# Modulation columns and first norm moved ahead of table work, and four short convolutions moved from TensorE to VectorE

## Chip, cores and metric

The kernel runs on one core of a Trainium2 chip. The metric is the device time of one execution in microseconds. TensorE (PE in the profile) does matrix products, VectorE (DVE) and ScalarE (ACT) elementwise work, GpSimd (POOL) elementwise work in SBUF, and SyncE (SP) issues most DMAs. Each runs its own queue of instructions in order and meets the others at semaphores.

## The reference

A 512-token sequence of width 1024 passes through three layers: a first block whose mixer is half S5 state space and half gated delta rule, followed by a routed mixture of experts; then a recurrent and windowed-attention layer and a Mamba-2 layer, each with a convolutional feed-forward part. The change lies at the start of the first block:

```python
mod = silu(c) @ w_ada + b_ada
sh1, sc1, gt1, sh2, sc2, gt2 = split(mod, 6)
a_in = rmsnorm(h, norm1_g) * (1 + sc1) + sh1
proj = a_in @ w_in
u_s5, qkv, z, a_gate, b_gate = split(proj, ...)

# S5, for each of its 2048 states
lam_bar = exp(lam * exp(log_step))
b_bar = (lam_bar - 1) / lam * b
states = scan(x -> lam_bar * x + b_bar u)
y = real(c states) + d_skip * u

# gated delta rule
qkv = silu(causal_depthwise_conv(qkv, conv_w))   # width 4, 1536 channels
q, k = l2norm(q) * 128 ** -0.5, l2norm(k)
```

## The kernel before

Activations lie with features on the partitions: h and u are 8 tiles (k = 0 to 7) of 128 features by the tokens. All weights of dense products come as units of 1 MB (16 blocks of 128x128) through a ring of four slots; SP loads a unit when the one that had its slot is used up (`load_unit`, L363). The order of work is written out by hand, one program per engine, and semaphores tie them together.

**The head, up to the first projection.** TensorE sums the squares of h for the norm (L497), then makes the first third of the modulation vector from eight units (`mod_unit`, L517) as rows; ScalarE copies them out (L1238) and TensorE transposes them (`mod_turned`, L524). VectorE meanwhile computes the S5 constants, a tile [128, 16] for each, then tables of the powers of the rotation, `fine` (16 entries, four doublings) and `coarse` (8 entries, three doublings), L1792 to L1813. After them it raises `s5_angle` to 2, which releases GpSimd (L2443). It then scales C into `cl5` (L1817 to L1828) and raises `s5_angle` to 3. Only then does it wait for `mod_turned` (L1831), add the bias (`mod_columns`), form the gain `modg`, and run `norm_apply(0, ...)`: for each k one scalar_tensor_tensor (L1681) and one tensor_scalar (L1675), with a drain between, one k overlapped with the next. Each k raises `normed`, and TensorE's first projection tile waits for each k (`out_tile`, L489). Last comes `bl_build(0)`, which makes four shifted versions of B for the first four S5 tiles.

GpSimd, from `s5_angle` 2 on, makes the sine and cosine tables of steps 0 and 1 (L2467 to L2475), then `cl_build` (the next four powers on C, L2450 to L2453), then the table of step j when VectorE has finished step j - 2.

**The projections.** TensorE does the four tiles of u_s5 with their reorder (`u4_turn`, L547), the gate columns (L562), and then 16 steps j. Step j: projection tile NS5 + j (12 tiles of q, k, v, then 4 of z), a convolution for 1 <= j <= PE_CONV, the S5 input product `s5_in` (L583), the turn of B for the next step `b4_turn` (L574), one unit of the rest of the modulation vector (L517), and in some steps an l2 sum (L623), `d4_in` (L594, in steps 2, 6, 10, 14) and `s5_out` (L610, in steps 4, 8, 12). VectorE's step j: a convolution for PE_CONV <= j < 12, the S5 scan of tile j (two TENSOR_TENSOR_SCAN at L1901 and ten products and sums around them), `bl_build` of the next four tiles in steps 1, 5 and 9, and `s5_result` in steps 5, 9, 13.

**The two ways of the convolution.** With i below PE_CONV (4) ScalarE first builds four diagonal 128x128 matrices of the taps (`conv_taps`, L1243) and copies the projection tile into the padded buffer `cbuf`; TensorE convolves by four matmuls with the shifted buffer (`conv_out`, L617) back into the tile's PSUM bank, and ScalarE takes the silu from there (L1248). With i from 4 on VectorE convolves, one tensor_scalar and three scalar_tensor_tensor (`conv`), and ScalarE takes the silu in place in SBUF (L1252). In both a square for the l2 norm follows when i < 8 (L1258). The lines that choose:

```python
if 1 <= j <= PE_CONV:                   # TensorE
    conv_out(j - 1)
...
if PE_CONV <= j < 12:                   # VectorE
    dve.wait_ge(sem("tile_read"), q0 + NS5 + j + 3)
    conv(qkv[:, j, :], cbuf[j % 2], CONV_C, ...)
```

A projection tile has one of two pairs of PSUM banks, and the tile after next needs its bank read (`tile_read`): by the silu for a tile that TensorE convolves, by the copy into `cbuf` for the others.

Of the kernel before, what the change touches and what calls it, by code (L numbers as in the profile page):

```python
# [26 lines left out]
ACT = mybir.ActivationFunctionType  # L27
AX = mybir.AxisListType.X

P = 128  # L30
# [34 lines left out]


CONV_C = 4
PE_CONV = 4
CONV_F = 3
LRU = 8  # L70
Q_HEADS = 16
# [105 lines left out]
def program(nc, a):  # L177
    with ExitStack() as ctx:
# [1024 lines left out]
        def _(act):  # L1203
# [90 lines left out]
            act.wait_ge(sem("pads_ready"), 1)  # L1294
            for j in range(16):
                q = q0 + NS5 + j
                if j == PE_CONV:
                    conv_silu(j - 1)
                act.wait_ge(sem("tile_done"), q + 1)
                if j < 12:  # L1300
                    if 2 <= j < PE_CONV + 2:
                        act.wait_ge(sem("conv_done"), j - 1)
                    if j >= PE_CONV + 2:
                        act.wait_ge(sem("conv_v"), j - PE_CONV - 1)
                    act.activation(cbuf[j % 2][:, 3:], pair(q), ACT.Copy
                                   ).then_inc(sem("conv_in" if j < PE_CONV else "tile_read"), 1)
                else:
                    act.activation(z1[:, j - 12, :], pair(q), ACT.Silu).then_inc(sem("tile_read"), 1)
                if j == 0:
                    b4_read(0)  # L1310
                if j + 1 < S5_TILES:
                    b4_read(j + 1)
                if 1 <= j < 13 and j != PE_CONV:
                    conv_silu(j - 1)
                if j + 1 >= 2 and j + 1 < PE_CONV:
                    conv_taps(j + 1)
                if j % 4 == 3:
                    d4_read(j // 4)
                if j == 11:
                    act.wait_ge(sem("squares_used"), DT + 8)  # L1320
                    act.wait_ge(sem("norm_applied"), 1)
                    act.activation(l2r, ps[0:8, 1, 0:SEQ], ACT.Sqrt, bias=eps[0:8, :]).then_inc(sem("l2_read"), 1)
# [315 lines left out]
            for n in range(len(SSD) + 3):  # L1638
                if n < len(SSD):
                    c, g = SSD[n]  # L1640
                    cnt, b = CH2[c][1], n % 2
                    act.wait_ge(sem("scan_in_done"), 16 + n + 1)
                    if n >= 2:
                        act.wait_ge(sem("scan_out_done"), 4 + n - 1)
                    bank = ps[:, 2 * b, :].rearrange("p (h n) -> p h n", h=4)
                    d = decay2[b][0:cnt, :, 0:cnt]
                    for e in range(4):
                        act.activation(d[:, e, :], bank[0:cnt, e, 0:cnt], ACT.Relu, scale=-1.0,
                                       bias=cs2[0:cnt, c, 4 * g + e:4 * g + e + 1])
                    if c:  # L1650
                        act.activation(eg2[b][:, :, 0:cnt], bank[:, :, 0:cnt], ACT.Exp).then_inc(sem("conv_in"), 1)
                    act.drain()
                    act.activation(d, d, ACT.Exp, scale=-1.0).then_inc(sem("scan_decay"), 1)
                if n >= 3:
                    group_square(n - 3)
# [17 lines left out]
        def _(dve):  # L1673
# [115 lines left out]
            for _ in range(2):  # L1789
                dve.drain()  # L1790
                doubled()
            for tab, size in ((fine, 16), (coarse, 8)):  # L1792
                dve.memset(tab[0][:, :, 0:1], 1.0)
                dve.memset(tab[1][:, :, 0:1], 0.0)
                n = 1
                while n < size:
                    dve.drain()
                    wc, ws = (S(x).unsqueeze(2).broadcast_to([P, S5_TILES, n]) for x in (15, 16))
                    t = [at(2048 + 256 * x, S5_TILES * n).rearrange("p (j n) -> p j n", n=n) for x in range(4)]
                    tt(t[0], tab[0][:, :, 0:n], wc, mul)  # L1800
                    tt(t[1], tab[1][:, :, 0:n], ws, mul)
                    tt(t[2], tab[0][:, :, 0:n], ws, mul)
                    tt(t[3], tab[1][:, :, 0:n], wc, mul)
                    tt(S(17), S(15), S(15), mul)
                    tt(S(18), S(16), S(16), mul)
                    tt(S(19), S(15), S(16), mul)
                    dve.drain()
                    tt(tab[0][:, :, n:2 * n], t[0], t[1], sub)
                    tt(tab[1][:, :, n:2 * n], t[2], t[3], add)
                    tt(S(15), S(17), S(18), sub)  # L1810
                    ts(S(16), S(19), 2.0, None, mul)
                    n *= 2
                dve.drain()  # L1813
            dve.drain().then_inc(sem("s5_angle"), 1)
            dve.wait_ge(sem("weights_loaded"), WEIGHTS)
            wide = lambda x: x.unsqueeze(2).broadcast_to([P, S5_TILES, 32])
# [10 lines left out]
                    ts(cl5[1][:, :, 0, :], t1, -1.0, None, mul)  # L1827
                dve.drain()  # L1828
            dve.drain().then_inc(sem("s5_angle"), 1)

            dve.wait_ge(sem("mod_turned"), 1)  # L1831
            def mod_columns(t0, tiles):

                turned = ps[:, 3, 256:256 + P].rearrange("p (o h r) -> p h r o", o=2, h=2)[:, :, 0:tiles // 2, :]
                out = mod[:, t0:t0 + tiles].rearrange("p (r o) -> p r o", o=2)
                tt(out, turned[:, 0], pcol("b_ada", t0, tiles).rearrange("p (r o) -> p r o", o=2), add)
                dve.drain()
                tt(out, turned[:, 1], out, add).then_inc(sem("mod_read"), 1)

            mod_columns(0, 16)  # L1840
            dve.drain()
            stt(modg[:, 0:DT], mod[:, DT:2 * DT], 1.0, pcol("norm1_g", 0, DT), add, mul)
            dve.drain()
            norm_apply(0, lambda k: modg[:, k:k + 1], lambda k: h[:, k, META:T2], lambda k: u[:, k, 0:SEQ], SEQ,
                       lambda k: mod[:, k:k + 1])

            def bl_build(t):

# [592 lines left out]
        def _(pool):  # L2441
# [98 lines left out]
            for n in range(len(CH2) * SSD_G + 2):  # L2540
                if n < len(CH2) * SSD_G:
                    c, g = n // SSD_G, n % SSD_G
                    (lo, cnt), b = CH2[c], n % 2
                    if n >= 2:
                        pool.wait_ge(sem("scan_out_done"), 4 + n - 1)
                    pool.wait_ge(sem("scan_scaled"), 16 + n + 1)
                    m = pool.tensor_tensor(xdd[0:cnt, b], xdt[n % 3][0:cnt], tail2[0:cnt, c, 4 * g:4 * g + 4].unsqueeze(2).broadcast_to(  # L2547
                        [cnt, 4, HEAD]), ALU.mult)
                    if c:
                        pool.wait_ge(sem("conv_in"), PE_CONV + n - SSD_G + 1)  # L2550
                        C = xbc[:, SSD_X + SSD_G + g, lo:lo + cnt]
                        m = pool.tensor_tensor(cdec[b][:, :, 0:cnt], eg2[b][:, :, 0:cnt], C.unsqueeze(1).broadcast_to([P, 4, cnt]),
                                               ALU.mult)
                    m.then_inc(sem("scan_pool"), 1)
# [145 lines left out]
```

## Time and profile before

| | |
|---|---|
| three runs | 3108.88, 3109.65, 3119.19 us |
| median | 3109.65 us |
| profiled execution | 3110.36 us |
| its span | 3108.5 us |
| TensorE busy | 2854.5 us, 92% |
| VectorE busy | 1035.6 us, 33% |
| ScalarE busy | 620.8 us, 20% |
| GpSimd busy | 268.8 us, 9% |

The span runs from the first to the last instruction of the profiled execution; 1.9 us of its time lie around it. Starts in rows are us from the span's beginning. A line in a row can be that of a helper: L1678 is VectorE's tensor_tensor, L1675 its tensor_scalar, L1681 its scalar_tensor_tensor, L489 every dense product of TensorE. The granted clock of TensorE is given as a share of full speed; 1.00 is 2.4 GHz and 0.50 is 1.2 GHz. The name `work` stands for the large buffer in which most tiles lie, `tmp` holds the padded buffers `cbuf`. A row of the order in time merges instructions of one form; its us run from the first one's start to the last one's end, and [16.50 <-DVE u L1675] says how long the engine was idle before it and who released it.

### The profile page before, as it was taken

To read this page: it belongs to the slowest core of one execution; us is meant where nothing else is said; L and a number is where in the kernel's file an instruction comes from. 1 tells how busy PE (TensorE), PEld (TensorE's weight loads), DVE (VectorE), ACT (ScalarE), POOL (GpSimd) and SP (SyncE) were. 2 spreads that over 40 slices of the span, in tenths; PEclk is the share of its full clock that TensorE was granted. 3 is DMA by queue.
4 is the path that set the end of the run, shared out by engine and by line. 5 is a ranking of instruction groups with operands and counts; after the bars stand their busy time and mean duration, and the time that the engine had idled before them with its cause. 6 is when DMAs were issued, how large, how long until landed. Compare 5 with 4: busy or idle time off the path is not lost.

```text
span 3108.5 us, 37906 instructions
## 1 busy us (share of the span) xinstructions
PE 2854.5 (92%) x14859; PEld 2136.6 (69%) x14859; DVE 1035.6 (33%) x2148; ACT 620.8 (20%) x1304; POOL 268.8 (9%) x368
## 2 busy tenths in 40 slices
PE   4999887678994999999999999999989899999998
PEld 2554683423332886687888788888877687888787
DVE  6355642311114342604333201113437604333202
ACT  1121220101112453602111001111127402111000
POOL 3121220011220000000000000000006400000000
PEclk7999998689997998999999999999978899999999
DMA  5133102478963111011212122122210011212122
GB/s 226 69 123 122 55 1 122 160 293 356 377 246 126 68 67 56 2 68 55 79 70 73 62 108 108 60 76 68 81 41 2 1 68 58 78 67 81 54 109 81
DMA packets 49449, 312.15 MB, mean 100 GB/s; under 512 B 12192, under 2 KB 14496, under 8 KB 18336
## 3 DMA queue, kind: packets, MB, share of 16 engines
q1 hardware_dynamic: 39520, 290.28, 24.5%
q0 software_dynamic: 9216, 17.85, 1.5%
q8 instruction: 98, 1.61, 0.2%
q10 hardware_dynamic: 576, 2.10, 0.2%
q14 instruction: 39, 0.32, 0.0%
HBM read 351.08 MB, written 16.78 MB: 118 GB/s over the span
## 4 chain that ended last, share of the span: by engine, by line
PE 65%; DVE 2%; ACT 1%; issue 0%; DVEq 0%; POOL 0%; POOLq 0%; ACTq 0%
PE ps L489 35%; PE ps L1001 18%; PE ps L1044 2%; PE ps L966 1%; PE ps L1168 1%; PE ps L984 1%; PE ps L952 1%; PE ps L1140 1%; PE ps L1163 1%; PE ps L991 1%; PE ps L1176 0%; PE ps L1195 0%; PE ps L897 0%; PE ps L1166 0%; PE ps L1118 0%
## 5 line engine op out<-in xcount | busy, mean ns | idle before, releaser
L489 PE MATMUL ps<-u,ring 128*128 128x264 f32 (+1 forms) x5248 | 1253.6, 401 | 27.4 <-DVE u L1675 20.7
L489 PEld LDWEIGHTS ps<-u,ring 128*128 128x128 f32 x5248 | 998.9, 191 | 272.5 <-issue 97.5
L1001 PE MATMUL ps<-work,ring 128*128 128x264 f32 x2432 | 557.6, 389 | 10.8 <-DVE work L1678 8.9
L1001 PEld LDWEIGHTS ps<-work,ring 128*128 128x128 f32 x2432 | 466.4, 192 | 93.5 <-DVE work L1678 9.7
L1675 DVE TENSOR_SCALAR work<-tmp,par 128x528 f32<-128x528 f32 (+2 forms) x136 | 74.9, 551 | 663.6 <-ACT tmp L1578 335.7
L1681 DVE SCALAR_TENSOR_TENSOR work<-tmp,par,work 128x528 f32<-128x528 f32 (+2 forms) x320 | 245.5, 767 | 50.0 <-issue 46.4
L829 PE MATMUL ps<-work,u 128*64 128x512 f32 x640 | 175.4, 615 | 32.3 <-DMA work<-in_experts,rs 30.1
L2285 DVE RECIPROCAL rs<-rs 128x264 f32<-128x264 f32 x8 | 14.4, 1803 | 529.7 <-ACT rs L1520 529.0
L1678 DVE TENSOR_TENSOR work<-work 128x128 f32<-128x128 f32 (+7 forms) x366 | 141.6, 425 | 62.2 <-ACT work L1450 18.4
L1578 ACT ACTIVATE tmp<-ps 128x528 f32<-128x528 f32 x80 | 48.9, 612 | 499.6 <-PE ps L489 499.6
L829 PEld LDWEIGHTS ps<-work,u 128*64 128x64 f32 x640 | 56.7, 142 | 109.5 <-issue 106.6
L2547 POOL TENSOR_TENSOR work<-u,work 128x256 f32<-128x256 f32 (+1 forms) x40 | 24.5, 612 | 1031.7 <-DVE u L1678 1011.1
L1527 ACT ACTIVATE sq<-ps 128x528 f32<-128x528 f32 x24 | 14.7, 611 | 432.0 <-PE ps L1001 432.0
L853 PE MATMUL ps<-work,ring 128*64 128x512 f32 x320 | 87.6, 598 | 0.5 <-DVE ring L2164 0.5
L1044 PE MATMUL ps<-u,ring 128*128 128x264 f32 x288 | 73.7, 407 | 13.4 <-DVE u L1681 13.4
L489 PE MATMUL ps<-work,ring 128*128 128x512 f32 x160 | 71.6, 610 | 12.7 <-DVE work L1678 11.0
L1044 PEld LDWEIGHTS ps<-u,ring 128*128 128x128 f32 x288 | 57.3, 201 | 26.3 <-DVE u L1681 10.2
L2164 DVE COPY ring<-ps 128x256 f32<-128x256 f32 x24 | 10.2, 424 | 175.5 <-PE ps L839 175.5
L489 PEld LDWEIGHTS ps<-work,ring 128*128 128x128 f32 x160 | 31.2, 196 | 52.5 <-issue 40.4
L1411 ACT ACTIVATE ring<-ps 128x256 f32<-128x256 f32 x24 | 9.2, 385 | 257.9 <-PE ps L829 257.9
L1604 ACT ACTIVATE tmp<-ps 128x528 f32<-128x528 f32 x32 | 19.6, 612 | 192.3 <-PE ps L489 192.3
L829 PE MATMUL ps<-ring,u 128*64 128x512 f32 x128 | 56.2, 592 | 0.0
(355 smaller groups left out, 2811.5 us busy)
## 6 DMA issues: line engine op xcount, KB each, us to landing
ring<-in_stream SPq DMA_DIRECT2D x169, 1024.0 KB, 4.8
work<-in_experts SPq DMA_DIRECT2D x25, 2048.0 KB, 14.5
work<-in_experts SPq DMA_DIRECT2D x25, 1024.0 KB, 9.3
ring<-in_experts SPq DMA_DIRECT2D x7, 2048.0 KB, 12.6
ring<-in_experts SPq DMA_DIRECT2D x7, 1024.0 KB, 8.7
work<-rows_out SPq DMA_DIRECT2D x4, 1024.0 KB, 8.0
h<-in_x_fm SPq DMA_DIRECT2D x1, 2048.0 KB, 10.7
rows_in<-work ACTq DMA_DIRECT2D x4, 512.0 KB, 2.6
```

What stands on the lines that cost most here:

```text
L489: m = pe.matmul(pair(q, half, cnt), ring[:, (n + b // 16) % WSLOTS, b % 16 * P:(b % 16 + 1) * P], x[:, lo:lo + cnt], start=(k == 0), stop= ...
L829: m = pe.matmul(ps[64 * e:64 * e + 64, p, :], xbt[p][:, k, 64 * e:64 * e + 64], mw[MSLOT[2 * s + e]][:, k * 512:(k + 1) * 512], start=(k = ...
L853: m = pe.matmul(ps[64 * e:64 * e + 64, 5 + half, :], ht_b[:, k, 64 * e:64 * e + 64], mw[MSLOT[2 * s + e]][:, w0:w0 + 512], start=(k == 0), ...
L952: m = pe.transpose(ps[0:kn, 4 + e, i * P:i * P + cnt], prob[0:cnt, n % 3, e, 1 + k0:1 + k0 + kn], ident[0:cnt, 0:cnt])
L966: m = pe.matmul(ps[64 * e:64 * e + 64, 6 + n % 2, 0:cnt], v_tok[0:kn, vc, 64 * kv:64 * kv + 64], prob_t[0:kn, n % 2, e, i * P:i * P + cnt] ...
L984: pe.matmul(ps[:, 6 + half, 0:HALF], ones, sq[:, i % 2, half * HALF:(half + 1) * HALF], start=first, stop=last).then_inc(sem("squares_used ...
L1001: return pe.matmul(pair(q0 + t, half, HALF), block(t, kk), rhs[kk][:, half * HALF:(half + 1) * HALF], start=(kk == 0), stop=(kk == parts - 1))
L1044: return pe.matmul(out, ring[:, (n0 + t // 2) % WSLOTS, b * P:(b + 1) * P], u[:, kk, half * HALF:(half + 1) * HALF], start=(kk == 0), stop ...
L1578: act.activation(halves(pad[e][:, 3:]), pair2(q0 + e), ACT.Copy).then_inc(sem("tile_read"), 1)
L1675: return dve.tensor_scalar(out, x, s1, s2, op0, op1) if op1 is not None else dve.tensor_scalar(out, x, s1, None, op0)
L1678: return dve.tensor_tensor(out, x, y, op)
L1681: return dve.scalar_tensor_tensor(out=out, in0=x, scalar=s, in1=y, op0=op0, op1=op1)
```

## The change

The doublings are split into two helpers, `table_start` and `table_double`. The first three doublings of `fine` stay in place; then come the modulation columns, the gain and the first norm; then the last doubling of `fine`, the three of `coarse`, and C. PE_CONV becomes 0, so the branch of VectorE takes all twelve tiles, and TensorE's branch and the tap matrices fall away. The SSD stage, much later, used `conv_in` with an offset of PE_CONV and now has a semaphore of its own.

```diff
--- before.py
+++ after.py
@@ -65,7 +65,7 @@
 
 
 CONV_C = 4
-PE_CONV = 4
+PE_CONV = 0
 CONV_F = 3
 LRU = 8
 Q_HEADS = 16
@@ -1294,7 +1294,7 @@
             act.wait_ge(sem("pads_ready"), 1)
             for j in range(16):
                 q = q0 + NS5 + j
-                if j == PE_CONV:
+                if j == PE_CONV and PE_CONV:
                     conv_silu(j - 1)
                 act.wait_ge(sem("tile_done"), q + 1)
                 if j < 12:
@@ -1648,7 +1648,7 @@
                         act.activation(d[:, e, :], bank[0:cnt, e, 0:cnt], ACT.Relu, scale=-1.0,
                                        bias=cs2[0:cnt, c, 4 * g + e:4 * g + e + 1])
                     if c:
-                        act.activation(eg2[b][:, :, 0:cnt], bank[:, :, 0:cnt], ACT.Exp).then_inc(sem("conv_in"), 1)
+                        act.activation(eg2[b][:, :, 0:cnt], bank[:, :, 0:cnt], ACT.Exp).then_inc(sem("ssd_eg"), 1)
                     act.drain()
                     act.activation(d, d, ACT.Exp, scale=-1.0).then_inc(sem("scan_decay"), 1)
                 if n >= 3:
@@ -1789,28 +1789,51 @@
             for _ in range(2):
                 dve.drain()
                 doubled()
-            for tab, size in ((fine, 16), (coarse, 8)):
+            def table_start(tab):
                 dve.memset(tab[0][:, :, 0:1], 1.0)
                 dve.memset(tab[1][:, :, 0:1], 0.0)
-                n = 1
-                while n < size:
-                    dve.drain()
-                    wc, ws = (S(x).unsqueeze(2).broadcast_to([P, S5_TILES, n]) for x in (15, 16))
-                    t = [at(2048 + 256 * x, S5_TILES * n).rearrange("p (j n) -> p j n", n=n) for x in range(4)]
-                    tt(t[0], tab[0][:, :, 0:n], wc, mul)
-                    tt(t[1], tab[1][:, :, 0:n], ws, mul)
-                    tt(t[2], tab[0][:, :, 0:n], ws, mul)
-                    tt(t[3], tab[1][:, :, 0:n], wc, mul)
-                    tt(S(17), S(15), S(15), mul)
-                    tt(S(18), S(16), S(16), mul)
-                    tt(S(19), S(15), S(16), mul)
-                    dve.drain()
-                    tt(tab[0][:, :, n:2 * n], t[0], t[1], sub)
-                    tt(tab[1][:, :, n:2 * n], t[2], t[3], add)
-                    tt(S(15), S(17), S(18), sub)
-                    ts(S(16), S(19), 2.0, None, mul)
-                    n *= 2
-                dve.drain()
+
+            def table_double(tab, n):
+                dve.drain()
+                wc, ws = (S(x).unsqueeze(2).broadcast_to([P, S5_TILES, n]) for x in (15, 16))
+                t = [at(2048 + 256 * x, S5_TILES * n).rearrange("p (j n) -> p j n", n=n) for x in range(4)]
+                tt(t[0], tab[0][:, :, 0:n], wc, mul)
+                tt(t[1], tab[1][:, :, 0:n], ws, mul)
+                tt(t[2], tab[0][:, :, 0:n], ws, mul)
+                tt(t[3], tab[1][:, :, 0:n], wc, mul)
+                tt(S(17), S(15), S(15), mul)
+                tt(S(18), S(16), S(16), mul)
+                tt(S(19), S(15), S(16), mul)
+                dve.drain()
+                tt(tab[0][:, :, n:2 * n], t[0], t[1], sub)
+                tt(tab[1][:, :, n:2 * n], t[2], t[3], add)
+                tt(S(15), S(17), S(18), sub)
+                ts(S(16), S(19), 2.0, None, mul)
+
+            table_start(fine)
+            table_start(coarse)
+            for n in (1, 2, 4):
+                table_double(fine, n)
+            dve.wait_ge(sem("mod_turned"), 1)
+            def mod_columns(t0, tiles):
+
+                turned = ps[:, 3, 256:256 + P].rearrange("p (o h r) -> p h r o", o=2, h=2)[:, :, 0:tiles // 2, :]
+                out = mod[:, t0:t0 + tiles].rearrange("p (r o) -> p r o", o=2)
+                tt(out, turned[:, 0], pcol("b_ada", t0, tiles).rearrange("p (r o) -> p r o", o=2), add)
+                dve.drain()
+                tt(out, turned[:, 1], out, add).then_inc(sem("mod_read"), 1)
+
+            mod_columns(0, 16)
+            dve.drain()
+            stt(modg[:, 0:DT], mod[:, DT:2 * DT], 1.0, pcol("norm1_g", 0, DT), add, mul)
+            dve.drain()
+            norm_apply(0, lambda k: modg[:, k:k + 1], lambda k: h[:, k, META:T2], lambda k: u[:, k, 0:SEQ], SEQ,
+                       lambda k: mod[:, k:k + 1])
+
+            table_double(fine, 8)
+            for n in (1, 2, 4):
+                table_double(coarse, n)
+            dve.drain()
             dve.drain().then_inc(sem("s5_angle"), 1)
             dve.wait_ge(sem("weights_loaded"), WEIGHTS)
             wide = lambda x: x.unsqueeze(2).broadcast_to([P, S5_TILES, 32])
@@ -1827,22 +1850,6 @@
                     ts(cl5[1][:, :, 0, :], t1, -1.0, None, mul)
                 dve.drain()
             dve.drain().then_inc(sem("s5_angle"), 1)
-
-            dve.wait_ge(sem("mod_turned"), 1)
-            def mod_columns(t0, tiles):
-
-                turned = ps[:, 3, 256:256 + P].rearrange("p (o h r) -> p h r o", o=2, h=2)[:, :, 0:tiles // 2, :]
-                out = mod[:, t0:t0 + tiles].rearrange("p (r o) -> p r o", o=2)
-                tt(out, turned[:, 0], pcol("b_ada", t0, tiles).rearrange("p (r o) -> p r o", o=2), add)
-                dve.drain()
-                tt(out, turned[:, 1], out, add).then_inc(sem("mod_read"), 1)
-
-            mod_columns(0, 16)
-            dve.drain()
-            stt(modg[:, 0:DT], mod[:, DT:2 * DT], 1.0, pcol("norm1_g", 0, DT), add, mul)
-            dve.drain()
-            norm_apply(0, lambda k: modg[:, k:k + 1], lambda k: h[:, k, META:T2], lambda k: u[:, k, 0:SEQ], SEQ,
-                       lambda k: mod[:, k:k + 1])
 
             def bl_build(t):
 
@@ -2547,7 +2554,7 @@
                     m = pool.tensor_tensor(xdd[0:cnt, b], xdt[n % 3][0:cnt], tail2[0:cnt, c, 4 * g:4 * g + 4].unsqueeze(2).broadcast_to(
                         [cnt, 4, HEAD]), ALU.mult)
                     if c:
-                        pool.wait_ge(sem("conv_in"), PE_CONV + n - SSD_G + 1)
+                        pool.wait_ge(sem("ssd_eg"), n - SSD_G + 1)
                         C = xbc[:, SSD_X + SSD_G + g, lo:lo + cnt]
                         m = pool.tensor_tensor(cdec[b][:, :, 0:cnt], eg2[b][:, :, 0:cnt], C.unsqueeze(1).broadcast_to([P, 4, cnt]),
                                                ALU.mult)
```

## Rows read from the trace of the kernel before

**Rows 1.** Page: its head line.

```profile
span 3108.5 us, 37906 instructions
```

**Rows 2.** Busy us of PE, PEld, DVE, ACT, POOL by stretch; clock, DMA share, GB/s.

```profile
58.00:78.00 20.00, 15.78 (x17) 4.31 (x16) 19.19 (x19) 0.21 (x1) 18.58 (x16) 0.50 0.00 0
184.00:320.00 136.00, 126.48 (x1014) 66.32 (x1005) 85.82 (x201) 27.59 (x52) 24.99 (x60) 0.96 0.32 128
```

**Rows 3.** Order in time, TensorE: start, us, line, form, count, [idle before].

```profile
57.33 2.05 PE L489 MATMUL ps<-u,ring 128*128 128x512 f32 x2 [16.50 <-DVE u L1675]
...
73.97 11.02 PE L489 MATMUL ps<-u,ring 128*128 128x512 f32 x20 [0.79 <-DVE u L1675]
...
116.81 8.38 PE L489 MATMUL ps<-u,ring 128*128 128x512 f32 x16
...
128.07 7.13 PE L489 MATMUL ps<-u,ring 128*128 128x512 f32 x16
135.04 3.60 PE L617 MATMUL ps<-tmp,work 128*128 128x512 f32 x8
138.48 0.61 PE L583 MATMUL ps<-work 128*128 128x128 f32 x4
...
141.78 7.11 PE L489 MATMUL ps<-u,ring 128*128 128x512 f32 x16 [1.47 <-ACT work L1248]
...
153.81 1.91 PE L594 MATMUL ps<-work 128*32 128x128 f32 x64
...
193.87 7.13 PE L489 MATMUL ps<-u,ring 128*128 128x512 f32 x16
...
206.42 1.91 PE L594 MATMUL ps<-work 128*32 128x128 f32 x64 [2.91 <-DVE work L1681]
```

**Rows 4.** Order in time, VectorE.

```profile
41.49 0.17 DVE L1675 TENSOR_SCALAR work<-work 128x16 f32<-128x16 f32 x1
...
48.21 5.08 DVE L1678 TENSOR_TENSOR work<-work 128x512 f32<-128x512 f32 x6 [0.17 <-issue]
...
54.00 0.17 DVE L1678 TENSOR_TENSOR mod<-ps,par 128x16 f32<-128x16 f32 x1 [0.17 <-issue]
...
54.80 1.78 DVE L1681 SCALAR_TENSOR_TENSOR u<-h,modg,rs 128x512 f32<-128x512 f32 x2
...
57.10 1.55 DVE L1681 SCALAR_TENSOR_TENSOR u<-h,modg,rs 128x512 f32<-128x512 f32 x1
...
76.30 13.62 DVE L1678 TENSOR_TENSOR work<-work 128x128 f32<-128x128 f32 x18
...
143.89 5.25 DVE L1678 TENSOR_TENSOR work<-work 128x128 f32<-128x128 f32 x18
...
182.93 0.49 DVE L1675 TENSOR_SCALAR work<-tmp,par 128x512 f32<-128x512 f32 x1 [11.71 <-ACT tmp L1305]
183.49 2.40 DVE L1681 SCALAR_TENSOR_TENSOR work<-tmp,par,work 128x512 f32<-128x512 f32 x3
...
188.22 1.79 DVE L1678 TENSOR_TENSOR work<-work 128x256 f32<-128x256 f32 x4
```

**Rows 5.** Order in time, GpSimd: first table, last product of C's powers.

```profile
48.20 0.40 POOL L2467 TENSOR_TENSOR work<-work 128x128 f32<-128x128 f32 x1 [47.74 <-DVEq L1814]
...
87.66 1.34 POOL L2453 TENSOR_TENSOR work<-work 128x512 f32<-128x512 f32 x1 [0.50 <-issue]
```

**Rows 6.** Order in time, VectorE: the second modulated norm, at 562 us.

```profile
562.53 1.41 DVE L1681 SCALAR_TENSOR_TENSOR u<-h,modg,rs 128x512 f32<-128x512 f32 x2
564.03 0.49 DVE L1675 TENSOR_SCALAR u<-u,mod 128x512 f32<-128x512 f32 x1
...
571.38 1.07 DVE L1675 TENSOR_SCALAR u<-u,mod 128x512 f32<-128x512 f32 x2
```

**Rows 7.** TensorE's busy us, granted clock, DMA share and GB/s by stretch.

```profile
44.00:48.00 4.00, 0.00 (x0) 0.53 0.39 164
78.00:82.00 4.00, 4.00 (x10) 0.95 0.00 0
```

## The prediction

> **What bounds the kernel now.** The page gives the span [rows 1]; the profiled execution took 3110.36 us against a median of 3109.65 for the three runs, so a sum made against it stands 0.7 us above the median. The change touches only the first 320 us, so I read that part: first the busy time by stretch, then each engine's order in time, then the granted clock.
>
> From 58 to 78 us TensorE is paced from outside: it runs at 0.50 of its clock (the 1.2 GHz level), while VectorE is busy 19.2 of 20 us and GpSimd 18.6 [rows 2]. TensorE stood idle for 16.5 us before its first projection matmul at 57.3, waiting for the normed u; each pair of matmuls for one k then takes 2.05 us and waits again for the next k, until 73.97 [rows 3]. Of the 20 matmuls from 73.97 to 85.0 the last 16 are tile 1 at its usual 7.1 us, so tile 0 ended at about 77.9. What VectorE did meanwhile: at 41.66 the third doubling of the fine table was over; then came the last doublings (to 48.2), C (to 54.0), the modulation columns, and the norm from 54.80 [rows 4]. The columns could have been had much earlier, since TensorE's last work before the gap ended at 40.8 (57.33 less 16.50), and their transpose lies before that end.
>
> Behind tile 0 TensorE has almost no gaps: five tiles to 125, then 16 steps j. So what ends tile 0 sooner, or leaves TensorE's own queue, shortens the run. From 184 to 320, where no convolution is left on TensorE, it is still busy 126 of 136 us and VectorE 86 [rows 2]: the engine that gets the work has room.
>
> **Part 1, columns and norm ahead of the last doublings and C.** No instruction is added, and no DMA is moved. VectorE reaches the columns at 41.66; with the 0.17 us of issue seen ahead of them and the 0.80 from 54.00 to 54.80 the norm starts at 42.6. Its price is not the old one: it ran beside GpSimd, which started its tables at 48.20 and went on to 89.0 [rows 5]. The second norm of the same shape ran alone: first normed column 1.99 us after its start (562.53 to 564.52), the whole in 9.92 (to 572.45) [rows 6]. A multiply that took 1.55 at 57.10 is 0.70 there. GpSimd is released by the end of the last doublings, which now come after the norm, so the norm is alone and I take the prices of rows 6. First column 44.6, first matmul about 44.8, last column 52.6 (before: near 75).
>
> TensorE's pair for one k takes 2.05 us at the low level and 0.89 (7.13 over 8) at the high one [rows 3]; a column comes every 1.2 us. The clock was down by a little after 44 (0.53 from 44 to 48) and came back 0.4 us into 78 to 82 [rows 7], after 4.4 us of matmuls without a gap from 73.97. In the new order the low level is slower than VectorE, so there is no gap from the start: two k at the low level (44.8 to 48.9), clock back near 49.2, six at 0.89, tile 0 over at 54.5. Bounds: 53.5 if the clock never falls, as the last column and one pair set it; 61.2 if it stays low for the whole tile (8 x 2.05 = 16.4). I take 54.5, as the nearest row for matmuls without gaps is the rise at 78.4. The weights of tile 0 are the first of the four units in flight at the end of the first loads, which are over by 46 (DMA share 0.39 from 44 to 48 [rows 7]): cost nothing, at most 1.2 us if they came last. **Gain 77.9 - 54.5 = 23.4 us** (24.4 to 16.7).
>
> What is late in its place. The last doublings take 6.55 us (41.66 to 48.21), C 5.79 (to 54.00): doublings over at 59.2, C at 65.0. Building the first B block then costs 5.3 us for its eighteen products alone (143.89) or 13.6 beside GpSimd (76.30) [rows 4]; I take the dear one and 1 us for its copies: over at 80. TensorE wants it after tile 4, before at 125.2, now at 102: 22 us in hand, cost nothing. If the cover were gone, each us beyond 102 would stand on the path. GpSimd starts at 59.2, 11 us later, and ends the build of C's powers at 100 instead of 89.0 [rows 5]; TensorE first wants those at d4_in of step 2, before at 153.8, now near 122: 22 us in hand again. On GpSimd the table of step 2 is queued behind that build, and VectorE wants it in that same step 2.
>
> **Part 2, four convolutions from TensorE to VectorE.** Each leaves TensorE 3.44 us sooner at the next work (135.04 to 138.48, L617 to L583): four make 13.8. Also leaving: the 1.47 us that tile 6's matmuls waited at 141.78 for ScalarE's silu to free the bank; ScalarE now copies the tile out and the bank is free at once. **Gain 13.8 + 1.5 = 15.2 us.** ScalarE loses 16 tap copies and gains four passes that read SBUF instead of PSUM; it is a fifth busy here: nothing. The SSD stage's semaphore has a new name and the same counts: nothing.
>
> VectorE gains four times 3.0 us (182.93 to 185.89: a multiply and three multiply-adds at 0.80); a step with its convolution takes 7.1 (182.93 to 190.01) [rows 4]. TensorE's steps 1 to 4 shrink to 8.8 (13.71 - 3.44 - 1.47), 10.5, 9.6 and 12.2. Step 1 also builds a B block (5.9): 13 us on VectorE, over 14 us after tile 1 of the loop; the block is wanted by b4_turn(4) in step 3, some 20 us after that tile. Behind it the convolution of step 2 starts 5 us late, and its silu is wanted one step later still; by step 4 the backlog is gone. The wait of 2.91 us at 206.42 (d4_in behind VectorE's result of the first four steps) has the same order on both sides and stays. Cost hidden, zero; from above it is bounded by rival C.
>
> **Sum:** 3110.4 - 23.4 - 15.2 = 3071.8 against the profiled execution, 3071 as a median. All behind 320 us waits on semaphores from this stage and moves up with it. The clock's phase can differ by a few us: tile 4, at 116.81, took 8.38 for 7.13 in a dip of the clock, and that dip may land elsewhere.
>
> **Rivals.** *A, the forecast*: 3071, with a spread of about 9 us for dips and repetition. Chance 0.73.
>
> *B, the clock stays low* through tile 0. For it: the old stretch ran low for 20 us at 80% busy. Against: those had gaps, the new has none. Price 61.2 - 54.5 = 6.7: **3078**. Chance 0.09.
>
> *C, the convolutions meet GpSimd.* Steps 0 to 3 overlap its table work partly; at the 1.55 us multiply-add of 57.10 a convolution costs some 5.8, and the B block 14.6. Step 1 is then 25 us on VectorE, over 25.5 after its tile, and b4_turn(4) waits 5.5: **3077**. Against: GpSimd makes one table a step and rests after it, and neither the convolution at 183.49 nor the products at 143.89 [rows 4] show a trace of it. Chance 0.07. The Trainium skill (GPSIMD Engine Reference, Key points) speaks for this rival: GpSimd shares its SBUF interfaces with VectorE and contends with VectorE instructions that have two SBUF inputs, which these multiply-adds have; taken for every convolution it gives C's time, and my sum takes it for none of them.
>
> *D, hidden anyway.* The B block or C's powers, pushed back by the norm, come 22 us later than I place them, and TensorE waits for them; only part 2 is left: 3110.4 - 15.2 = **3095**, inside 0.5% (15.5 us, what a measurement here can tell from no change). Against: twice 22 us in hand. Chance 0.07.
>
> *E, slower.* The wide matmuls of the convolutions leave steps 1 to 4 with more small ones and waits, and the clock falls in the loop. A tile then takes 16.4 for 7.1, so 9.3 us a step; from the fifth such step on the gain of 38.6 is gone, and with the clock low in eight of sixteen the time is 3071 + 74 = **3145**. For it: the dip before tile 4. Against: from 184 to 320 the same steps without convolutions hold 0.96 [rows 2]. Chance 0.04.
>
> That the change doesn't do what it says is within D: if the silu or the columns still waited for what was removed.
>
> **Numbers.** Faster by over 0.5%: A + B + C = 0.89. Within: D = 0.07. Slower: E = 0.04. The range takes A with its spread, B and C, and B with the low clock lasting into tile 1 (one more 9.3, 3087): 3062 to 3087.
>
> **What would show it.** Right: columns near 41.8, norm's multiplies at 0.70 to 0.75, first projection matmul near 45, tile 0 over near 54.5, GpSimd's first table near 59, no L617, step 1 to 2 in 8.8 us, VectorE's convolutions of tiles 0 to 3 at 3.0. Wrong: a clock of 0.50 beyond 50 (B), a wait of TensorE on VectorE in step 3 (C), one before b4_turn(0) or the first d4_in (D), a clock under 0.9 between 100 and 160 beyond the old dip (E). A later stage that is not shorter or longer by itself would leave the difference equal to that at the end of this stage.

## The result, and the profile after

Four runs each: the changed kernel takes 3070.87 us in the median (3066.54 to 3075.64), the kernel before 3112.62 (3108.88 to 3119.19). The ratio is 0.9866 with a 95% interval of 0.9844 to 0.9887, a gain of 41.7 us with some 7 to either side. The prediction was 3071, with a range of 3062 to 3087. In a second comparison (run v0 below) the changed kernel took 3064.34 us and the kernel before 3104.86, 40.5 us apart. The profiled execution took 3069.59 us; its span of 3067.8 is 40.7 under the old one.

VectorE's order in time, where the columns and the norm now stand (the rows answering to [rows 4] and [rows 6]):

```profile
41.57 0.17 DVE L1678 TENSOR_TENSOR mod<-ps,par 128x16 f32<-128x16 f32 x1
...
42.34 1.42 DVE L1681 SCALAR_TENSOR_TENSOR u<-h,modg,rs 128x512 f32<-128x512 f32 x2
43.83 0.49 DVE L1675 TENSOR_SCALAR u<-u,mod 128x512 f32<-128x512 f32 x1
...
51.18 1.07 DVE L1675 TENSOR_SCALAR u<-u,mod 128x512 f32<-128x512 f32 x2
...
59.05 5.10 DVE L1678 TENSOR_TENSOR work<-work 128x512 f32<-128x512 f32 x6 [0.17 <-issue]
...
65.33 13.39 DVE L1678 TENSOR_TENSOR work<-work 128x128 f32<-128x128 f32 x18
99.80 0.49 DVE L1675 TENSOR_SCALAR work<-tmp,par 128x512 f32<-128x512 f32 x1 [21.09 <-ACT tmp L1305]
```

The norm starts at 42.34 and its last column is out at 52.25, 9.9 us, as the second norm had it. C and the first B block (over at 78.7) follow, and then VectorE is idle for 21 us until the first convolution.

TensorE's order in time (the rows answering to [rows 3]):

```profile
44.46 16.11 PE L489 MATMUL ps<-u,ring 128*128 128x512 f32 x32 [2.91 <-DVE u L1675]
60.50 2.02 PE L547 MATMUL ps<-work,con 128*32 128x128 f32 x32
...
80.46 9.42 PE L562 MATMUL ps<-work,u 128*128 128x8 f32 x64
89.81 2.03 PE L547 MATMUL ps<-work,con 128*32 128x128 f32 x32
91.77 7.30 PE L489 MATMUL ps<-u,ring 128*128 128x512 f32 x16
...
100.10 0.71 PE L583 MATMUL ps<-work 128*128 128x128 f32 x4 [0.80 <-ACT work L1264]
...
101.97 7.13 PE L489 MATMUL ps<-u,ring 128*128 128x512 f32 x16
...
110.70 7.13 PE L489 MATMUL ps<-u,ring 128*128 128x512 f32 x16
...
152.52 7.13 PE L489 MATMUL ps<-u,ring 128*128 128x512 f32 x16
...
165.07 1.91 PE L594 MATMUL ps<-work 128*32 128x128 f32 x64 [2.90 <-DVE work L1681]
```

Two projection tiles are over at 60.57, so with 7.13 for the second, tile 0 ended at 53.4. The same reading of the kernel before (84.99 less 7.13) gives 77.9; both tiles were over 24.4 us sooner. Step 1 begins at 101.97 and step 2 at 110.70: 8.7 us, and no L617 stands between them. The wait of 2.90 at d4_in is where it was, 41.35 us sooner.

Where the 40.7 us of the profiled pair stand, by the same instruction in both traces: tile 0 over, 24.4 us sooner; the first s5_in (L583), 26.1; d4_in of step 6, 41.35; the transpose that ends the stage (L524, 324.79 against 280.20), 44.6; the first attention product of the next layer (L966), 45.8; the first L1001 behind it, 42.2; the end, 40.7. So the head gave 26, the convolutions' steps 15.2 and a shorter fall of the clock another 3.3: from tile 12 to tile 13 it is 16.2 us against 19.4. Later stages took 4 back. Most of that is one stretch. In the kernel before, by stretch (its length, TensorE's busy time and count, granted clock, DMA share, GB/s):

```profile
1217.90:1313.60 95.70, 92.35 (x782) 0.80 0.01 1
```

and in the changed kernel:

```profile
1172.20:1271.40 99.20, 95.95 (x781) 0.77 0.01 1
```

The matmuls are the same, the clock is 0.77 against 0.80, and the stretch is 3.5 us longer. This loss does not belong to the change: in a second profile of the changed kernel (run v0 below, 3062.41 us) the same stretch took 95.8 us at 0.80, as in the kernel before.

### The profile page after: what moved, and what is told of

It reads as the page before. It is cut to its first block, busy times and chain, and to the rows that moved or that the text cites. A ratio compares the mean times of both kernels' runs of the same rounds, so it can differ in the third digit from the quotient of the medians.

```text
span 3067.8 us, 37853 instructions
## 1 busy us (share of the span) xinstructions
PE 2837.5 (92%) x14827; PEld 2131.3 (69%) x14827; DVE 1035.3 (34%) x2164; ACT 616.3 (20%) x1288; POOL 267.4 (9%) x368
## 4 chain that ended last, share of the span: by engine, by line
PE 66%; DVE 2%; ACT 1%; issue 0%; DVEq 0%; POOL 0%; POOLq 0%; ACTq 0%
PE ps L489 36%; PE ps L1001 18%; PE ps L1044 2%; PE ps L966 1%; PE ps L952 1%; PE ps L1168 1%; PE ps L984 1%; PE ps L1140 1%; PE ps L1163 1%; PE ps L991 1%; PE ps L1176 0%; PE ps L1195 0%; PE ps L897 0%; PE ps L1166 0%; PE ps L932 0%; PE ps L1118 0%
## 5 line engine op out<-in xcount | busy, mean ns | idle before, releaser
L1001 PE MATMUL ps<-work,ring 128*128 128x264 f32 x2432 | 558.7, 390 | 10.8 <-DVE work L1678 8.9
L1001 PEld LDWEIGHTS ps<-work,ring 128*128 128x128 f32 x2432 | 467.1, 192 | 93.8 <-DVE work L1678 9.7
L1681 DVE SCALAR_TENSOR_TENSOR work<-tmp,par,work 128x528 f32<-128x528 f32 (+2 forms) x332 | 254.6, 767 | 50.9 <-issue 46.4
L1044 PE MATMUL ps<-u,ring 128*128 128x264 f32 x288 | 74.1, 409 | 13.4 <-DVE u L1681 13.4
L1044 PEld LDWEIGHTS ps<-u,ring 128*128 128x128 f32 x288 | 57.5, 202 | 26.6 <-DVE u L1681 10.2
L489 PEld LDWEIGHTS ps<-work,ring 128*128 128x128 f32 x160 | 31.2, 197 | 52.3 <-issue 40.5
```

The source lines that it names most:

```text
L489: m = pe.matmul(pair(q, half, cnt), ring[:, (n + b // 16) % WSLOTS, b % 16 * P:(b % 16 + 1) * P], x[:, lo:lo + cnt], start=(k == 0), stop= ...
L1001: return pe.matmul(pair(q0 + t, half, HALF), block(t, kk), rhs[kk][:, half * HALF:(half + 1) * HALF], start=(kk == 0), stop=(kk == parts - 1))
L1044: return pe.matmul(out, ring[:, (n0 + t // 2) % WSLOTS, b * P:(b + 1) * P], u[:, kk, half * HALF:(half + 1) * HALF], start=(kk == 0), stop ...
L1681: return dve.scalar_tensor_tensor(out=out, in0=x, scalar=s, in1=y, op0=op0, op1=op1)
```

## The experiments

### The two parts apart

The order alone, in the changed kernel:

```diff
-PE_CONV = 0
+PE_CONV = 4
```

> The new order with the four convolutions left on TensorE (PE_CONV = 4). Theory, the two parts act in different places and add up: tile 0 of the projections ends near 53.5 us as in the changed kernel, the steps keep their four blocks of 3.44 us and the wait of 1.47 us, and the time is 15 us above the changed kernel, 3086, some 26 under the kernel before. Rival 1, the order alone is hidden behind the convolutions' stage: at most 5 us under before, 3108 or more. Rival 2, the convolutions' move brings nothing once the order is changed: 3071.

Measured: 3083.87 us (five runs) against 3110.43 before; ratio 0.9909 (0.9895 to 0.9923), 26.6 us. Its first s5_in comes 22.2 us sooner than before, not 26: tile 0 was over at 54.1, 0.6 us behind the changed kernel, and the clock fell for longer in the gates: they and tile 4 took 11.75 and 8.27 us, against 9.42 and 7.30.

The convolutions alone, in the kernel before:

```diff
-PE_CONV = 4
+PE_CONV = 0
...
-                if j == PE_CONV:
+                if j == PE_CONV and PE_CONV:
```

(and the SSD stage's semaphore as in the change).

> The old order with all twelve convolutions on VectorE. Theory: 15 us under the kernel before, 3097 to 3098, tile 0 still ending near 77.9 us, step 1 to 2 in 8.8 us instead of 13.7. Rival, the convolutions fit on VectorE only because the new order has freed it: a wait of TensorE on VectorE of 2 us or more in steps 1 to 4 and a gain under 8 us.

Measured: 3095.64 against 3110.43; ratio 0.9954 (0.9939 to 0.9968), 14.8 us. TensorE's waits from 100 to 320 us:

```profile
PE ps L594 <- DVE work L1681: 5.8, 2, 2.9
PE ps L630 <- DVE rs L1915: 2.3, 1, 2.3
PE ps L610 <- DVE work L1678: 1.7, 1, 1.7
PE ps L489 <- issue: 1.7, 1, 1.7
PE ps L583 <- ACT work L1264: 0.8, 1, 0.8
```

These are the waits of before without the 1.47 on ScalarE: VectorE takes the four convolutions in the old order too. 26.6 and 14.8 make 41.4, the whole 41.7. Each gain is uncertain by more than 4 us, so that the sum agrees within 0.3 is luck: in the traces the end of the stage comes 22.2 us sooner with the order alone, 18.7 with the convolutions alone and 44.6 with both. That is 3.7 us short of adding up, nearly all of it the 3.9 us that the order alone lost in tile 0, the gates and tile 4. But each part brings its own gain without the other, and the rivals that made one depend on the other fall.

Two convolutions on TensorE, in the new order (PE_CONV = 2):

> The new order with two of the four convolutions on TensorE (PE_CONV = 2). Theory, each convolution is worth its 3.44 us on TensorE and the bank wait of 1.47 us comes once, with the first of them: 6.9 + 1.5 = 8.4 us over the changed kernel, 3079. Rival, the gain comes with the last one only (the whole chain of copies, taps and silu on ScalarE has to go): within 2 us of 3086.

Measured: 3081.55 (3076.48 to 3085.19), ratio 0.9912 (0.9896 to 0.9927). The total, with a spread of 9 us, cannot tell the theory's 3079 from the rival's 3084 to 3088; the trace can. At the first s5_in it is 26.0 us ahead of the kernel before, at d4_in of step 2, behind the two convolutions that stay, still 26.0, and at the first s5_out (L610, step 4) 32.9: 6.9 us for the two that left, 3.44 each. The 1.47 us wait is still there. The changed kernel had 41.3 at that place, 8.4 more. That is the theory's number. The totals agree less. In the later steps the clock took 2 us back here and gave 3.3 in the changed kernel; the rest of the difference lies behind the stage.

### What the norm costs beside GpSimd

In the changed kernel GpSimd starts only at 59.05, behind the norm. Here it is given unused work from the time of the transpose: 14 multiplies of 128x512 as shown, and in two further runs 36 of 128x128 or 22 of 128x256:

```diff
+            pool.wait_ge(sem("inputs_loaded"), INPUTS)
+            pool.wait_ge(sem("mod_turned"), 1)
+            for _ in range(14):
+                pool.tensor_tensor(clt[0]..., con[:, 0:512], con[:, 512:1024], ALU.mult)
+                pool.drain()
             pool.wait_ge(sem("s5_angle"), 2)
```

> The changed kernel, with GpSimd made to multiply 128x512 constants (14 times, into its own scratch, results unused) beside the norm. Theory, half of part 1 is the earlier start (12.5 us) and half the norm's own price, which GpSimd had doubled: the norm takes 18 to 20 us again instead of 9.9, its multiplies 1.5 us instead of 0.75, TensorE's clock stays low or comes late since there are gaps between the columns, and tile 0 ends 8 to 12 us later than 53.4, so the time is 3078 to 3083. Rival, the old norm was slow for another reason (its inputs, or its place behind C): norm 10 to 11 us, tile 0 at 53 to 55, no change of time.

> The same with GpSimd at 128x128 multiplies (36 of them, a similar stretch of time). Theory, a VectorE instruction waits for the GpSimd instruction that is under way, so its cost goes with the length of GpSimd's: multiplies of the norm near 0.9 to 1.1 us, the norm 11 to 14 us, tile 0 at 54 to 58. Rival, the two share bandwidth element by element: the price depends on how much of the time GpSimd is busy and not on the size of its instructions, so the norm is within 10% of the one beside 128x512 multiplies.

> The changed kernel, with GpSimd at 22 multiplies of 128x256 beside the norm. Theory, instructions of the two engines take turns, one VectorE instruction for each of GpSimd's: with 128x512 (1.50 us each) one k of the norm took 3.08, two turns; with 128x128 (0.68 us) 1.46, just over two turns. With 128x256 (0.95 to 1.0 us) a k takes 1.9 to 2.1 us and tile 0 ends at 58 to 61. Rival, each VectorE instruction waits on average for half of GpSimd's: a k takes 1.6 to 1.8.

Order in time of VectorE beside 128x512 multiplies:

```profile
46.03 3.51 DVE L1681 SCALAR_TENSOR_TENSOR u<-h,modg,rs 128x512 f32<-128x512 f32 x2
49.62 1.33 DVE L1675 TENSOR_SCALAR u<-u,mod 128x512 f32<-128x512 f32 x1
50.87 1.75 DVE L1681 SCALAR_TENSOR_TENSOR u<-h,modg,rs 128x512 f32<-128x512 f32 x1
...
53.95 1.75 DVE L1681 SCALAR_TENSOR_TENSOR u<-h,modg,rs 128x512 f32<-128x512 f32 x1
```

and of GpSimd in that run:

```profile
40.38 20.93 POOL L2453 TENSOR_TENSOR work<-con 128x512 f32<-128x512 f32 x14 [39.92 <-PE ps L524]
```

VectorE beside 128x256 multiplies:

```profile
47.99 1.21 DVE L1681 SCALAR_TENSOR_TENSOR u<-h,modg,rs 128x512 f32<-128x512 f32 x1
49.27 0.79 DVE L1675 TENSOR_SCALAR u<-u,mod 128x512 f32<-128x512 f32 x1
49.98 1.21 DVE L1681 SCALAR_TENSOR_TENSOR u<-h,modg,rs 128x512 f32<-128x512 f32 x1
```

and GpSimd:

```profile
39.44 21.19 POOL L2453 TENSOR_TENSOR work<-con 128x256 f32<-128x256 f32 x22 [38.98 <-PE ps L524]
```

VectorE beside 128x128 multiplies:

```profile
46.03 0.94 DVE L1681 SCALAR_TENSOR_TENSOR u<-h,modg,rs 128x512 f32<-128x512 f32 x1
47.05 0.52 DVE L1675 TENSOR_SCALAR u<-u,mod 128x512 f32<-128x512 f32 x1
47.49 0.94 DVE L1681 SCALAR_TENSOR_TENSOR u<-h,modg,rs 128x512 f32<-128x512 f32 x1
```

and GpSimd:

```profile
40.55 19.61 POOL L2453 TENSOR_TENSOR work<-con 128x128 f32<-128x128 f32 x29 [40.09 <-PE ps L524]
```

Divide each stretch of GpSimd by its count, and set it beside the time from one k of the norm to the next (two VectorE instructions):

| GpSimd's instruction | one of them | one k of the norm | two of GpSimd's | norm in all | tile 0 over |
|---|---|---|---|---|---|
| none | | 1.22 | | 9.9 | 53.4 |
| 128x128, unused | 0.68 | 1.46 | 1.35 | 11.6 | 56.6 |
| 128x256, unused | 0.96 | 2.00 | 1.93 | 16.2 | 61.8 |
| 128x512, unused | 1.50 | 3.08 | 2.99 | 19.4 | 66.9 |
| 128x512, kernel before | 1.39 | 2.78 | 2.79 | 20.3 | 77.9 |

(With 128x512 GpSimd's work ended at 61.3, before the norm, so its total is less than eight times 3.08 and a start.) GpSimd is busy all the time in each, yet the price goes from 0.24 to 1.9 us a k: it is set by the size of GpSimd's instructions. A k takes two turns of GpSimd, one for each VectorE instruction, within about 0.1 us in every row. The last row is the kernel before itself, where GpSimd builds the powers of C beside the norm (12 instructions from 57.06 to 73.77 us, five k from 57.10 to 70.98). Its two engines start by turns:

```profile
59.70 1.27 POOL L2453 TENSOR_TENSOR work<-work 128x512 f32<-128x512 f32 x1
59.76 1.75 DVE L1681 SCALAR_TENSOR_TENSOR u<-h,modg,rs 128x512 f32<-128x512 f32 x1
...
61.10 1.31 POOL L2450 TENSOR_TENSOR work<-work 128x512 f32<-128x512 f32 x1
61.59 1.11 DVE L1675 TENSOR_SCALAR u<-u,mod 128x512 f32<-128x512 f32 x1
62.38 1.22 POOL L2451 TENSOR_TENSOR work<-work 128x512 f32<-128x512 f32 x1
```

That the engines take turns instruction by instruction is the reading that foretold the 128x256 row, and the order of the rows shows it; what makes them do so no run here shows. Short instructions do not each wait for a turn: the ten 128x64 products ahead of the columns took 4.65 us beside 128x512 multiplies, for 1.41 alone, the length of three GpSimd instructions and not of ten. By the Trainium skill (GPSIMD Engine Reference, Key points) GpSimd shares its SBUF interfaces with VectorE, in contention with instructions of two SBUF inputs and those in a 2-port mode. The slower scalar_tensor_tensor (0.75 alone, 1.75 here) agrees with the first of these; the tensor_scalar has one SBUF input and is slower too (0.49 alone, 1.33 here), which fits only if it runs in such a mode, and that no run here shows.

The times were 3083.02 (128x512), 3074.42 (128x128) and 3082.61 (128x256), one execution each. The first and the last are alike although tile 0 was over 5 us apart: with 128x256 the gates and tile 4 took 20.0 us for 16.7 at a lower clock, and both runs end the stage at 293.6. The price of the norm is read from the trace, not from the total. Tile 0 came a little later than expected in both: 13.4 us behind the changed kernel for 8 to 12 with 128x512, and at 61.8 for 58 to 61 with 128x256.

Of the 24.4 us by which tile 0 came sooner, 13.4 are lost again when GpSimd works beside the norm in large instructions (66.9 against 53.4), but 3.7 of these are the third doubling and the columns ahead of the norm, which had no such company in the kernel before. From the two kernels themselves: the norm starts 12.5 us sooner (42.34 for 54.80), takes 10.4 less (9.9 for 20.3), and TensorE ends tile 0 1.6 us closer behind its last column.

### How much the pushed-back work had in hand

Unused multiplies on VectorE, ten or 22, ahead of the first build of B:

```diff
+            for _ in range(10):
+                stt(p5[0], con[:, 0:SEQ], 1.0, con[:, SEQ:2 * SEQ], mul, mul)
+                dve.drain()
             dve.wait_ge(sem("s5_turned_read"), 1)
```

> The changed kernel with ten unused multiplies of 128x512 on VectorE ahead of the first build of B, 8 to 15 us of work. Theory, the pushed-back work had some 20 us in hand (the build ends at 78.7, TensorE wants it at 98.9): no change of time, the first turn of B still follows tile 4 without a wait. Rival, VectorE's chain was already on the path: the time grows by the added work, 8 us or more.

> The same with 22 of them, 25 to 33 us of work if GpSimd makes them slow, 18 if not. Theory: the 20 us in hand are used up and TensorE waits for the build of B by what is over them, 0 to 12 us, and that wait is seen in front of the first turn of B (L574). Together with the run of ten this brackets the slack. Rival as before: over 18 us.

With ten: 3070.57. VectorE's order in time:

```profile
65.10 11.53 DVE L1681 SCALAR_TENSOR_TENSOR work<-con 128x512 f32<-128x512 f32 x10 [0.17 <-issue]
...
78.05 16.99 DVE L1678 TENSOR_TENSOR work<-work 128x128 f32<-128x128 f32 x18
```

The build was over at 95.0 instead of 78.7, and the first s5_in still came at 100.38 (100.10 in the changed kernel). With 22: 3079.71, and TensorE:

```profile
106.22 0.69 PE L574 MATMUL ps<-con,work 128*128 128x128 f32 x2 [7.17 <-DVEq L1870]
107.39 1.22 PE L583 MATMUL ps<-work 128*128 128x128 f32 x4 [0.47 <-ACT work L1264]
...
108.96 1.94 PE L517 MATMUL ps<-ring,work 128*32 128x128 f32 x32
```

A wait of 7.2 us, in the place named. And more: behind it the clock is at its lower level (s5_in 1.22 for 0.71, L517 1.94 for 1.08), so that by d4_in of step 2 the loss is 9.7 and at the end of the stage 14.5; the whole execution is only 9.1 us longer than with ten, one execution each. The build was over at 106.1, 27.4 us later than in the changed kernel, and TensorE waited 7.2 of them: 20.2 us were in hand, as said. In this stage the wait cost more than its length, because the clock came down with it.

### A wait removed, and what took its place

VectorE's s5_result ahead of bl_build in steps 5 and 9:

```diff
+                if j % 4 == 1 and j > 4:
+                    s5_result(j // 4 - 1)
                 if j % 4 == 1 and j < 12:
                     bl_build(j // 4 + 1)
...
-                if j % 4 == 1 and j > 4:
-                    s5_result(j // 4 - 1)
```

> The changed kernel with VectorE's s5_result put ahead of bl_build in steps 5 and 9 (in 13 there is no build). Theory, the two waits of 2.9 us of TensorE at d4_in (steps 6 and 10) come from the 5.9 us build that stands before the result on VectorE; with the result first both go and the time is 5 to 6 us lower, 3065. Rival 1, the build is then late for b4_turn in steps 7 and 11: the waits move there, no gain. Rival 2, the stage's time is given back in a later stage through the clock, so that the run shows under 2 us.

> The changed kernel itself, to stand beside the two versions below on one chip. Theory: 0.9866 of the kernel before within 0.002, the end of the 16 steps at 280 us. Where its dips of the clock fall between 200 and 240 us may differ from the profile seen.

> The result ahead of the build, a second time. In its first profile both waits of 2.9 us were gone, but a stretch of low clock fell on the steps 11 and 12 and the stage ended only 2.5 us sooner. Theory: the waits are worth 5.8 us and the dip is another matter, so over several executions the time is 4 to 6 us under the changed kernel. Rival: taking the waits away moves the dip onto busier work each time, and 0 to 3 us stay.

The first time: 3066.03 against 3106.43 before (0.9864). Side by side on one chip: the changed kernel 3064.34 (0.9869, 0.985 to 0.9887), this version 3064.66 (0.9865, 0.9847 to 0.9883). The totals show no difference, and both expectations (5 to 6 us, then 4 to 6) missed. Yet both waits of 2.9 us are gone from its trace. TensorE in three stretches of the changed kernel (length, busy time and count, granted clock, DMA share, GB/s):

```profile
80.00:96.00 16.00, 16.00 (x118) 0.79 0.15 58
205.00:217.00 12.00, 9.10 (x112) 0.86 0.01 2
222.00:236.00 14.00, 11.68 (x91) 1.00 0.57 226
```

and of this version, in its second run:

```profile
80.00:96.00 16.00, 16.00 (x118) 0.79 0.16 62
205.00:217.00 12.00, 12.00 (x114) 1.00 0.18 59
222.00:236.00 14.00, 11.55 (x128) 0.63 0.06 25
```

In the changed kernel the fall of the clock came with the wait at 208 and cost 1.6 us (d4_in 2.82 for 1.91, the tile 7.85 for 7.13). Without it the clock falls at step 12 instead, at the 2.5 us wait for the l2 root and the small products around it. The changed kernel has this wait too (2.32 us), and its clock stays at 1.00 there. TensorE's order in time in this version's first run (these took 1.08, 1.12 and 2.84 us in the changed kernel):

```profile
228.20 1.94 PE L517 MATMUL ps<-ring,work 128*32 128x128 f32 x32
230.06 2.07 PE L630 MATMUL ps<-rs,con 8*128 8x512 f32 x2
232.06 4.71 PE L610 MATMUL ps<-work 128*32 128x128 f32 x96
```

From tile 12 to tile 13 it is 21.1 us against 16.2. So 5.8 + 1.6 - 4.9 = 2.5 us, which is what the stage ended sooner (277.7 against 280.2), and again 2.8 in the second pair. The rival that the dip moves onto busier work held: it did so in both traces of this version. What is left, 2 to 3 us, is below what the totals can show: of the two profiled pairs one ends 2.9 us sooner than the changed kernel and one 3.6 later, by differences of later stages.

Last, that version with the gates dealt out and the third doubling behind the norm as well:

```diff
                 if t:
                     u4_turn(t - 1)
-
-            for c in range(CHUNKS):
                 for k in range(DT):
-                    m = pe.matmul(ps[:, 3, 384 + 8 * c:392 + 8 * c], u[:, k, c * P:(c + 1) * P], ...
+                    m = pe.matmul(ps[:, 3, 384 + 8 * t:392 + 8 * t], u[:, k, t * P:(t + 1) * P], ...
...
-            for n in (1, 2, 4):
+            for n in (1, 2):
                 table_double(fine, n)
...
-            table_double(fine, 8)
+            for n in (4, 8):
+                table_double(fine, n)
```

> v1, with the 64 gate matmuls of 8 columns dealt out behind the four first tiles, 16 to each, and the third doubling of the fine table put behind the norm too. Theory: the clock fell in the gates because for some 9 us TensorE had nothing but 8-column matmuls; dealt out between tiles they leave it up, so the 64 take 7 to 7.5 us in place of 9.4 and the dip before tile 4 is gone (2.4 us); the columns start at 40.3 instead of 41.6 (1.2 us). 3 to 4 us under v1. Rival: the clock falls at that place for another reason (the time since the start, the reads of u) and the dip stays between 80 and 95 us.

Measured: 3055.74 (five runs), ratio 0.9842 (0.9825 to 0.9859), against 3064.34 for the changed kernel and 3064.66 for v1 on the same chip. That is 8.9 us under v1, where 3 to 4 were expected; at the end of the stage it is 5.4. The intervals against the kernel before still overlap; of the runs themselves the slowest here (3061.64) is under the fastest there (3062.41). The gate matmuls from 50 to 95 us (busy, mean ns, idle before):

```profile
L560 PE MATMUL ps<-work,u 128*128 128x8 f32 x64 | 7.7, 256 | 0.0
```

and two of its stretches:

```profile
60.00:96.00 36.00, 36.00 (x229) 1.00 0.16 59
...
216.00:230.00 14.00, 11.64 (x120) 0.88 0.34 141
```

The 64 gate matmuls take 7.7 us instead of 9.4 to 9.6, the clock stays at 1.00 from 60 to 96 (0.91 in the changed kernel on this chip), and tile 4 starts at 89.83 instead of 91.87. The earlier columns brought nothing: the norm started at 41.66, but tile 0 was over at 53.9, no sooner than in the changed kernel. The rest of the stage's 8.2 us (271.9 against 280.1) is the two waits, less a fall at step 12 that is shorter than in v1 (tile 12 to 13 in 17.8 us, for 21.1 there and 16.2 in the changed kernel).

## Why the prediction was right, and what it missed

The forecast A held: the same two parts gave the gain, each near its price. It forecast 38.6 us less than the profiled execution before; the profiled pair measured 40.7 and the medians 41.7. That the median lies within 0.2 us of 3071 is luck, since the kernel before read 3112.62 here instead of the 3109.65 that the sum started from, and the four runs of the changed kernel lie 9 us apart. By its steps:

- Columns at 41.57 (said 41.8), norm 9.9 us, last column 52.25 (52.6). **Right**, and the norm's own price (20.3 us beside GpSimd, 9.9 alone) was 10.4 of the 24.4 us.
- Tile 0 over at 53.4; said 54.5, from a clock that comes back at 49.2. The clock was 0.57 of full from 44 to 48 and 1.00 from 48 to 52: it rose sooner than said, so TensorE caught up with the last column, at the lower bound of the text. The gain was 24.4, not 23.4.
- C over at 64.7 (65.0), the B block at 78.7 (80), GpSimd's first table at 59.05 (59.2), TensorE's demand at 98.9 (102), the last power of C at 96.8 (100). **Right**: rival D would have needed 20 us more, and the runs of ten and 22 put the edge at 20.2, between delays of 16.3 us (no wait) and 27.4 (a wait of 7.2).
- For four convolutions 13.8 and the bank wait 1.5: measured 15.25 us between the first s5_in and d4_in of step 6, in the changed kernel, and 15.2 in the run with the convolutions alone. **Right**. The wait of 2.91 stayed, as said.
- Rival C fell: the convolution of tile 3 at 130.40 took 2.44 for its three multiply-adds while GpSimd made a table, and no wait appears in step 3. The two engines did meet there, but GpSimd paid: its products took 0.67 to 0.87 us, for 0.40 to 0.45 in the tables of the two steps before.
- Rival E fell: from 94 to 182 us the clock is 1.00 throughout. What it feared is seen elsewhere, in the runs with 22 multiplies and with the result first, but not at the size that it priced.
- **The term that was mis-sized** is the last of the sum, "the clock's phase can differ by a few us" with no value in it. It was worth 1.7 us before the first s5_in (gates and tile 4: 18.40 before, 16.72 after), 3.3 in step 12, and minus 4 later: 1 us in all in this pair, by cancelling. The minus 4 was that execution's alone. The 3.3 came with the convolutions' removal in both orders (190.1 us from the first to the last matmul of s5_in with four on TensorE, 171.6 without; 18.5 and not 15.2), while with two removed 4.9 us went instead of 6.9. What sets where the clock falls stays open: in these traces it fell at or soon behind waits of 2.3 to 7.2 us with small matmuls around them, and in 64 matmuls of 8 columns in a row. But in the changed kernel the wait of 2.90 us in step 6 passed without a fall (d4_in 1.91) where the same wait in step 10 did not (2.82), and so did that of 2.32 us in step 12.

## What to carry to other kernels

Ask what the other engine is doing beside a critical elementwise stretch: moving the norm out from beside GpSimd was worth nearly as much (10.4 us) as starting it sooner (12.5). Beside this norm GpSimd's company was cheap in small instructions and dear in large ones. A few us of waiting taken from TensorE count only if the clock does not fall somewhere else in exchange; compare the granted clock by stretch before believing the wait's length, and deal small matmuls out among large ones.

## What the runs showed of the hardware

VectorE's 128x512 instructions and GpSimd's went turn by turn: one k of the norm, two instructions, took 1.46, 2.00 and 3.08 us beside GpSimd instructions of 0.68, 0.96 and 1.50 us, and 2.78 beside those of 1.39 in the kernel before. A single-input tensor_scalar waited like the two-input scalar_tensor_tensor (1.33 us for 0.49, 1.75 for 0.75).

The granted clock fell inside a stretch where the profile shows no idle time of TensorE: 64 matmuls of 8 columns, 0.79 from 80 to 96 us with 16.00 of 16 us busy, and the same matmuls in four lots of 16 kept it at 1.00. Weight loads filled that time (9.55 of 10 us from 80 to 90, against 8.01 of 18 from 60 to 78 at 1.00). The clock also fell with waits, though not with each: after 7.2 us without work the next products took 1.22 for 0.71 us and 1.94 for 1.08.
